# Operand buffer b_buf at 32 bytes, in place of 64, past a multiple of 512 bytes from the weights' buffers

## The reference

```python
# block 1: stick-breaking attention, then a squared-ReLU MLP
a = rms_norm(h, norm_mix)
qkv = a @ w_qkv                      # 2048 x 6144
h = h + attention(qkv) @ w_o         # 2048 x 2048
h = h + square(relu(rms_norm(h) @ w1)) @ w2      # 2048 x 8192, 8192 x 2048
# block 2 (16 meta tokens in front): pooling and convolution branches, gates, gated MLP
proj = rms_norm(h) @ w_in            # 2048 x 12288
y_a = pool(u) @ pool_w * pool_scale
y_b = (gb * conv(gc * v)) @ conv_out_w
h = h + (g_a * y_a + g_b * y_b) @ w_o2
gate, up = split(rms_norm(h) @ w_gate_up)        # 2048 x 11264
h = h + (silu(gate) * up) @ w_down               # 5632 x 2048
out = rms_norm(h)[:, 16:]
```

## Time and profile before

| | |
|---|---|
| median of 3 executions | 2597.28 us (2597.19 to 2597.47) |
| span of the profiled execution, first to last instruction | 2596.2 us |
| the profiled execution's own time | not listed apart; the median lies 1.1 us above the span |
| PE busy | 2584.7 us, 16053 matmuls |
| DVE, ACT, POOL busy | 1614.3, 1174.4, 141.7 us |
| DMA | 485.26 MB, 187 GB/s |
| mean granted TensorE clock | 0.999 of full speed |

### The profile page before, as it was taken

The page is one execution under the profiler, slowest core; times in us unless marked ns, Lnnn a source line. Parts: engine busy times, 40 slices in busy tenths (PEclk is TensorE's granted clock), DMA queues, the critical chain, the costliest instruction groups (busy, mean ns, idle before and its releaser), DMA issues.

```text
span 2596.2 us, 40378 instructions
## 1 busy us (share of the span) xinstructions
PE 2584.7 (100%) x16053; PEld 2323.9 (90%) x16053; DVE 1614.3 (62%) x1398; ACT 1174.4 (45%) x1181; POOL 141.7 (5%) x87
## 2 busy tenths in 40 slices
PE   9999999999999999999999999999999999999998
PEld 9999998888888888899899988888888888888887
DVE  6577766655556556786654776566756555554555
ACT  5455554434434444544443344444544434443444
POOL 0000100000000000000200530000000000000001
PEclk9999999999999999999999999999999999999999
DMA  7554455555555555555555555555555555555563
GB/s 260 182 170 157 163 182 189 188 188 192 190 185 191 192 184 191 183 190 179 187 186 178 182 191 189 183 194 194 186 187 194 178 194 195 185 191 192 192 210 130
DMA packets 243954, 485.26 MB, mean 187 GB/s; under 512 B 7728, under 2 KB 8944, under 8 KB 243696
## 3 DMA queue, kind: packets, MB, share of 16 engines
q1 hardware_dynamic: 243520, 483.12, 55.7%
q10 hardware_dynamic: 320, 0.53, 0.1%
HBM read 481.53 MB, written 2.10 MB: 186 GB/s over the span
## 4 chain that ended last, share of the span: by engine, by line
PE 98%; DVE 1%; DMA 0%; ACT 0%; issue 0%; POOL 0%; SPq 0%; DVEq 0%; POOLq 0%; ACTq 0%
PE ps L1322 42%; PE ps L1329 21%; PE ps L1369 14%; PE ps L1350 8%; PE ps L1377 7%; PE ps L1356 4%; PE ps L1425 0%; PE ps L1479 0%; DMA raw<-in_sb_w_qkv_dram 0%; PE ps L1391 0%; PE ps L1413 0%; PE ps L1484 0%; PE ps L1462 0%; PE ps L1416 0%; DVE wlo L768 0%
## 5 line engine op out<-in xcount | busy, mean ns | idle before, releaser
L768 DVE TENSOR_TENSOR wlo<-raw,whi 128x1024 fp32r<-128x1024 f32 x900 | 1107.3, 1261 | 928.6 <-ACT whi L561 928.5
L561 ACT ACTIVATE whi<-raw 128x1024 fp32r<-128x1024 f32 x900 | 919.4, 1054 | 1330.7 <-PE ps L1329 899.2
L1322 PE MATMUL ps<-b_buf,whi 128*128 128x512 f32 x2688 | 643.7, 392 | 0.0
L1322 PEld LDWEIGHTS ps<-b_buf,whi 128*128 128x128 f32 x2688 | 492.9, 188 | 97.6
L1322 PE MATMUL ps<-a_buf,whi 128*128 128x512 f32 x1792 | 434.0, 394 | 0.0
L1322 PEld LDWEIGHTS ps<-a_buf,whi 128*128 128x128 f32 x1792 | 329.2, 188 | 69.2
L1329 PEld LDWEIGHTS ps<-b_buf,wlo 128*128 128x128 f32 x2688 | 335.1, 188 | 14.0
L1329 PE MATMUL ps<-b_buf,wlo 128*128 128x256 f32 x2688 | 338.2, 278 | 0.0
L1369 PE MATMUL ps<-a_buf,whi 128*128 128x258 f32 (+4 forms) x2560 | 330.9, 282 | 1.0 <-ACT a_buf L578 1.0
L1369 PEld LDWEIGHTS ps<-a_buf,whi 128*128 128x128 f32 x2560 | 315.7, 188 | 1.5 <-ACT a_buf L578 1.2
L1329 PEld LDWEIGHTS ps<-a_buf,wlo 128*128 128x128 f32 x1792 | 226.6, 188 | 9.6
(11 more groups left out here) (202 smaller groups left out, 1399.3 us busy)
## 6 DMA issues: line engine op xcount, KB each, us to landing
raw<-in_mlp_w_dram SPq DMA_DIRECT2D x128, 1024.0 KB, 5.1
raw<-in_w_in_dram SPq DMA_DIRECT2D x96, 1024.0 KB, 5.0
raw<-in_w_gate_up_dram SPq DMA_DIRECT2D x88, 1024.0 KB, 4.9
raw<-in_sb_w_qkv_dram SPq DMA_DIRECT2D x44, 1024.0 KB, 5.0
raw<-in_w_down_dram SPq DMA_DIRECT2D x44, 1024.0 KB, 5.1
raw<-in_sb_w_o_dram SPq DMA_DIRECT2D x16, 1024.0 KB, 5.1
raw<-in_conv_out_w_dram SPq DMA_DIRECT2D x16, 1024.0 KB, 5.1
raw<-in_w_o_dram SPq DMA_DIRECT2D x16, 1024.0 KB, 5.1
```

The costliest lines, as they stand in the source:

```text
L561: act.activation(whi[:, unit_of(n, u)], raw[:, n % RAW, u * UK:(u + 1) * UK, :], ACT.Copy).then_inc(w_hi, 1)
L768: dve.tensor_tensor(wlo[:, s], raw[:, n % RAW, u * UK:(u + 1) * UK, :], cast(whi[:, s]), ALU.subtract).then_inc(w_lo, 1)
L1322: pe.matmul(ps[:, 4 * half + j, :].rearrange("p (a n) -> p a n", a=2), whi[:, s, kt, j * P:(j + 1) * P], buf[:, :, x, tok], start=c == 0 a ...
```

## The change

One number in the placement. `b_buf` begins 32 bytes earlier, and with it all that is placed behind it: `h`, `full`, `U`, `S1`, `S2`, `acc`, the small vectors, `ident`, `negtri`, and the region of `za`, `G`, `k_hi`, `v_hi`, `pp` and `y_tok`. `raw`, `whi`, `wlo`, `a_buf`, `c_buf` and `d_buf` stay where they are. Distances among the buffers that move together stay the same.

```diff
         a_buf, a_off = place("a_buf", [P, 2, NT, TW], F32R)
         c_buf, _ = place("c_buf", [P, 2, NT, T], F32R, at=a_off + 64)
         d_buf, _ = place("d_buf", [P, 2, NT, T], F32R, at=a_off)
-        top[0] += 64
+        top[0] += 32
         b_buf, b_off = place("b_buf", [P, 2, NT, T], F32R)
```

## The result

| | before | changed |
|---|---|---|
| median | 2597.32 us (2597.19 to 2597.47, 4 runs) | 2610.69 us (2610.46 to 2611.72, 4 runs) |
| span of the profiled execution | 2596.2 us | 2608.7 us (own time 2610.46 us) |
| ratio to before | | 1.0053, 95% interval 1.0041 to 1.0065 |

The kernel became 13.4 us slower. The time lies inside the stated range of 2587 to 2614 us, but 9 us above the forecast itself, outside the forecast's own range of 2593 to 2607, and 1 us from rival C.

The account below looks back on a forecast made before the run. PE was taken as the bound: 16053 matmuls back to back, the time being the sum of their spacings. Terms +3.8 - 1.2 + 1.6 = +4.2 us gave 2601.5 us, +0.16%; range 2587 to 2614 us, the forecast's own 2593 to 2607.

Parts of the forecast that it names:

- rival C: Paired line 1322 on `b_buf` slower, 234 ns, the two streams meeting in each matmul: 2611.7 us, +0.56%; chance 0.24.
- Term 1: Moved buffers' reads and writes by VectorE, ScalarE and GpSimd: costed at nothing, 1 us at most.
- Terms 2 and 3: Attention, whose distances stay the same, and panels on `a_buf`, `c_buf`, `d_buf`, whose operands stay: nothing for either.
- Term 4: 2688 matmuls of line 1329 on `b_buf`, 256 columns: from 115.3 to 116.7 ns, +3.8 us.
- Term 5: 960 unpaired matmuls on `b_buf`: from 117.9 ns to the scores' 116.7 ns, -1.2 us.
- Term 6: 2688 paired matmuls of line 1322 on `b_buf`: from 229.4 to 230 ns, +1.6 us.
- The bound of 235 ns: High bound for line 1322 on `b_buf`, from the dearest `a_buf` tile: +15.1 us.
- Rival A: Matmul spacing doesn't depend on the distance, so no effect: 2597.3 us; chance 0.14.
- Rival B: Paired line 1322 on `b_buf` becomes clean, 226.7 ns, -7.3 us: 2588.8 us, -0.33%; chance 0.20.
- threshold of +1 ns a matmul: Extra cost per paired matmul, over the 230 ns taken, from which the slower rival was said to decide.
- the bound of 5.2 us: Difference from no change that a measurement of this kernel can tell, about 0.2%.

Follow-up runs that it names:

- experiment 1: Kernel before with only `b_buf` 32 bytes earlier and everything behind it left in its old place: 2611.05 us, ratio 1.0051.
- experiment 4: Kernel before with `b_buf` and `c_buf` at other distances from the weights' buffers, two distances per kernel, five kernels: 2608.42 to 2622.64 us.
- experiment 3: Changed kernel with one constant stationary tile for line 1322 on `b_buf`, 64 or 32 bytes from `b_buf` modulo 256: 2602.66 and 2611.88 us.
- experiment 2: Kernel before with every buffer, the weights' too, 32 bytes further on, all distances kept: 2597.31 us, ratio 0.9999.

## Why the prediction was right or wrong

**What came, by the prediction's own classes**: slower, to which it gave 0.36. Its forecast, the same within 0.2%, had 0.42 and did not come. The time lies in the stated range because that range was drawn to take in rival C, not because the sum was right.

**That the kernel is a row of spacings, and nothing else can move the time**: right. The spacings on `b_buf` give +13.7 us where the time rose by 13.4.

**Term 1, the moved buffers at nothing**: right, shown by experiment 1 (2611.05 us without their move). **Terms 2 and 3**: right; the lines of attention changed by less than 0.1 us together, and lines 1322 and 1329 on `a_buf` and `c_buf` by less than 0.1 ns a matmul. What changed on `b_buf` was not handed on to those panels.

**Term 4, line 1329 at 116.7 ns by the scores**: right in number, 116.69, but in part by luck. The pattern is another one: line 1329 goes 117, 117, 116, the scores go 118, 120, 113, 116, and the same price from the same rows missed in term 5. The term was +3.8 us and measured +2.7, because its present value was read as 115.3 ns from two pieces where all 2688 give 115.69. That reading took the alternation of two rounded rows for strict; by the starts, 79 of the 168 pieces are of the cheap kind (113.3 ns on average) and the others at 117.8 ns.

**Term 5, -1.2 us**: measured +0.1. Line 1369 did not fall to the scores' 116.7 ns but stayed at 117.76. Its runs of 16, and those of 8 on line 1377, fell mostly into threes (118, 119 and 116 ns).

**Term 6, line 1322 at 230 ns, +1.6 us**: wrong in size; this is the step that failed. It measured 233.40 ns, +10.9 us, and its error of 9.3 us is the whole miss, since those of terms 4 and 5, 1.1 us too much and 1.3 us too little, cancel. The step took the mean of the neighbours: 64 and 256 bytes on `a_buf` were both at 230 ns, and 32 lies between. The sweep shows that there is no between: 0, 32, 64 and 96 give 228.4, 233.4, 229.3 and 233.4 ns. The prediction had named this as a sign of being wrong, a state at 32 that none of its neighbours has, and it came; a piece of 16 took 3.73 us, where 3.68 was forecast and 3.74 was C's. The tile rows were a weak base besides, as each tile of `a_buf` has only four matmuls, and experiment 4 shows five passing before a run at 0 settles. The bound of 235 ns did hold it.

**Rival A, no effect**: fell, by experiments 1 and 3. The Trainium skill, "SBUF — State Buffer", section "Who interferes with whom", has PE's port for the moving operand and its port for LDWEIGHTS independent of each other, and PE never waiting on anyone. Of ScalarE and VectorE the traces bear that out: in the changed kernel line 1322 took 233.3 ns with those engines idle, and the same to within 0.1 ns, at the same places in a piece, with them at work on the weights' buffers. That PE's own two operands don't touch each other they do not bear out: with all else equal the line took 229.65 or 233.42 ns by the place of its stationary tile (experiment 3).

**Rival B** did not come. **Rival C** came: 234 ns for line 1322 was its price, and 2611.7 us its time. Part of that closeness is the same cancelling of terms 4 and 5, and so luck. Its threshold of +1 ns a matmul was also set too high: above the sum's +4.2 us the bound of 5.2 us is reached with 0.4 ns. I gave it 0.24 although two things spoke for it, the dearer tiles at 128 and 192 and the `u2` rows. The distances of `u2` are 32, 96, 160 and 224, so those rows were the nearest in the trace to the new place. It is not the half line that makes them dear: experiment 2 moved them by 32 bytes, and line 1369 of `u2` took 122.02 ns as before. But they say little of 32 in the paired form, and the unpaired line on `b_buf` did not become dearer at 32. What should have raised the chance is simpler: of the four distances in a period that the earlier trace rows show, two were dear, and a distance without a row is as likely to be one of that kind as of the other.

What stays open is what happens inside one spacing: why 256 bytes is the period, and what rule picks the pattern. The runs show which patterns occur at which distance and after which neighbour, not the circuit. That the two streams meet at the memory is inferred from experiments 2 and 3. They show that the stationary tile's place against the moving one decides, and that ScalarE's and VectorE's accesses do not. Whether a gap of a few cycles between moving stream and load would end it was not tried.

## What to carry to other kernels

When matmuls run back to back and their spacing is some per cent above the columns over the clock, compare the spacing between groups of like shape that read different buffers. If it differs, the distance between moving and stationary tiles is a free parameter. Here it was worth 25 us of 2600 between the best and the worst of the six distances of `b_buf` (modulo 256) that were tried. `c_buf` had moved too in the dearest of these kernels, which is 0.8 us of the 25. The kernel as it stood, at 64, was the best. Sweep it on the whole kernel and measure each value: neither the neighbouring distances nor the sum over separate lines foretold the next one here. And when another buffer is put in front of such operands, keep the distance.

## What the runs showed of the hardware

- The spacing of fp32r matmuls depends on the distance of moving and stationary tile, by up to 6 ns at 512 moving columns, and repeats every 256 bytes: 233.40 and 233.38 ns at 32 and 288.
- Even in the cleanest pattern 512 moving columns take 226.7 ns and 256 take 113.3, at a granted clock of 0.999 of 2.4 GHz; 213.3 and 106.7 are the columns alone, so each takes a sixteenth more. No line of over a hundred matmuls averaged less than 226.6 or, its waits left out, 113.3 in any kernel.
- A pattern lasts as long as the run of like matmuls, and which one is entered is handed on: line 1322 with `whi` at 64 took 229.33 or 233.43 ns, as `wlo` lay at 64 or 192.
- It repeats closely. The medians of two kernels with all distances equal were 2597.31 and 2597.38 us.
